# Four of ten expert blocks per group added on chip by 0/1 products instead of by a scatter to DRAM

## The reference, cut to what matters

```python
act = silu(einsum('nd,edf->nef', t, w_gate_e)) * einsum('nd,edf->nef', t, w_up_e) * gates[:, :, None]
routed = einsum('nef,efd->nd', act, w_down_e)           # 64 experts, inner width 256, 8 gates per token not zero
x = x + gate_ffn * (routed + shared)                    # then a last RMSNorm
```

## Time and profile before

| what | value |
|---|---|
| median of 3 executions | 1000.14 us (999.35 to 1002.08) |
| profiled execution, its own time | 997.12 us |
| its span | 995.4 us |
| PE busy | 873.0 us (88%) |
| DVE, ACT, POOL busy | 340.7, 249.2, 157.0 us |
| moved by DMA | 299.40 MB, mean 301 GB/s |
| `gate_up` of turn 11 / turn 39 starts | 527.19 us / 951.03 us |

### The profile page before, as it was taken

One profiled execution on the slowest core, in us unless ns is written; L12 is line 12 of the kernel. 1 busy time (PEld: TensorE's weight loads), 2 busy tenths in 40 slices (PEclk: granted clock), 3 DMA queues, 4 the chain that ended last, 5 costly groups with the idle time before them and its releaser, 6 DMA issues.

```text
span 995.4 us, 11581 instructions
## 1 busy us (share of the span) xinstructions
PE 873.0 (88%) x4026; PEld 495.0 (50%) x4026; DVE 340.7 (34%) x833; ACT 249.2 (25%) x415; POOL 157.0 (16%) x210
## 2 busy tenths in 40 slices
PE   4799998999999899999987787978979888978974
PEld 2388876899888744443333332423324333433321
DVE  1653572766674552332321212111112121212125
ACT  2546623444233411112110111111101111111111
POOL 7200000000010500221221111111212212212212
PEclk9799999999999999999997989978979998989998
DMA  9974887232346688899999999999999999999924
GB/s 344 348 272 149 290 299 172 86 105 85 108 137 234 247 343 305 301 358 380 405 388 408 374 376 391 356 369 387 359 376 368 378 383 384 363 375 391 385 65 190
DMA packets 87048, 299.40 MB, mean 301 GB/s; under 512 B 18181, under 2 KB 34625, under 8 KB 62048
## 3 DMA queue, kind: packets, MB, share of 16 engines
q1 hardware_dynamic: 64400, 263.21, 67.0%
q0 software_dynamic: 13904, 31.13, 11.6%
q10 hardware_dynamic: 8704, 4.54, 1.9%
HBM read 287.16 MB, written 29.10 MB: 318 GB/s over the span
## 4 chain that ended last, share of the span: by engine, by line
PE 48%; DMA 37%; SPq 5%; DVE 4%; issue 2%; ACT 2%; POOL 1%; ACTq 1%; POOLq 0%; DVEq 0%
DMA gu<-in_w_up_e_dram 33%; PE bank L1423 14%; PE bank L1047 6%; PE bank L1049 6%; PE bank L1048 6%; PE bank L1442 4%; SPq L484 4%; DMA chunk_raw<-in_w_ada_dram 3%; PE bank L1316 2%; PE bank L1075 2%; PE bank L1116 1%; DMA y_dram<-y_sb,slot_row 1%; SPq L495 1%; PE bank L1411 1%; PE bank L1149 1%
## 5 line engine op out<-in xcount | busy, mean ns | idle before, releaser
L1423 PE MATMUL bank<-gu,x_t 128*64 128x512 f32 (+1 forms) x1024 | 311.3, 654 | 72.3 <-DMA gu<-in_w_up_e_dram 70.6
L1423 PEld LDWEIGHTS bank<-gu,x_t 128*64 128x64 f32 (+1 forms) x1024 | 109.7, 163 | 242.2 <-issue 215.7
L1442 PE MATMUL bank<-dn,a_t 128*64 128x512 f32 (+1 forms) x512 | 145.3, 597 | 4.8 <-ACT shared_sb L982 3.5
L719 POOL DMA_INDIRECT y_dram<-y_sb,slot_row x39 | 62.7, 1608 | 463.3 <-issue 237.8
L1904 DVE TENSOR_TENSOR act_sb<-silu_sb,bank 128x256 f32<-128x256 f32 x40 | 16.9, 422 | 323.8 <-ACT silu_sb L1017 323.8
L1017 ACT ACTIVATE silu_sb<-bank 128x256 f32<-128x256 f32 x40 | 15.4, 385 | 344.3 <-PE bank L1423 344.3
L1442 PEld LDWEIGHTS bank<-dn,a_t 128*64 128x64 f32 (+1 forms) x512 | 48.5, 150 | 74.8 <-issue 67.5
L1047 PE MATMUL bank<-h_hi,chunk_lo 128*128 128x384 f32 x240 | 84.6, 353 | 0.0
L1008 ACT ACTIVATE y_sb<-bank,slot_gate 128x512 f32<-128x512 f32 x80 | 50.7, 684 | 126.1 <-PE bank L1442 103.2
L1049 PE MATMUL bank<-h_hi,chunk_hi 128*128 128x384 f32 x240 | 81.1, 338 | 0.0
L1048 PE MATMUL bank<-h_lo,chunk_hi 128*128 128x384 f32 x240 | 80.8, 337 | 0.0
(11 more groups left out here) (336 smaller groups left out, 939.4 us busy)
## 6 DMA issues: line engine op xcount, KB each, us to landing
gu<-in_w_gate_e_dram SPq DMA_DIRECT2D x64, 1024.0 KB, 16.0
gu<-in_w_up_e_dram SPq DMA_DIRECT2D x64, 1024.0 KB, 28.2
dn<-in_w_down_e_dram SPq DMA_DIRECT2D x64, 1024.0 KB, 27.2
chunk_raw<-in_w_ada_dram SPq DMA_DIRECT2D x24, 1024.0 KB, 8.6
chunk_raw<-in_w_in_dram SPq DMA_DIRECT2D x18, 1024.0 KB, 5.3
chunk_raw<-in_w_out_dram SPq DMA_DIRECT2D x4, 1024.0 KB, 5.0
y_dram<-zeros POOLq DMA_DIRECT2D x1, 3072.0 KB, 18.0
chunk_raw<-in_w_pa_dram SPq DMA_DIRECT2D x2, 1024.0 KB, 5.0
```

Of the source, the lines that this page charges most:

```text
L719: pool.indirect_dma_start(y_dram[:, :], bass.IndirectOffsetOnAxis(ap=slot_row[:, u % UN:u % UN + 1], axis=0), y_sb[u % 2][:, :], None, bou ...
L1423: mm = pe.matmul(bank[2 + u % 2][at_x, :].rearrange("p (g n) -> p g n", g=2), x_t[:, cols], wide[:, :, k, :], start=(k == 0), stop=(k == K ...
L1442: mm = pe.matmul(bank[5 + half][at_x, :], a_t[:, cols], dn[slot_of(x, first)][:, wc], start=(k == 0), stop=(k == 1))
```

## The change

In the three later groups the blocks u = 0, 2, 5 and 7 (`PLACED`) are no longer scattered: 12 blocks of 40. In the turn after such a block, behind everything else of that turn, DVE makes its 0/1 matrix `place_t` in one operation over 384 columns (it compares `tok_no`, the numbers 0 to 383, with the block's `slot_val`). PE waits for it, then runs six products `place_t` x `y_sb` into six accumulator banks, and DVE adds each of the six banks to `ffn_acc`, three tiles of 128x1024 in SBUF. PE's next `gate_up` waits for the first of these additions, `turn_tokens` after it for the sixth. POOL fills `ffn_acc` with zeros and makes `tok_no` in the last turn of the first group. After the loop, DVE multiplies each tile of `ffn_acc` by `gate_ffn` and adds it to `x_sb`, six operations of 128x1024 in a row, ahead of L1926. The counts in the waits on `added` follow: 27 scatters instead of 39. The semaphores of the three RMS steps are merged into `squares_summed` and `rstd_made`, with counts that keep each wait as it was (left out below).

```diff
+PLACED = (0, 2, 5, 7)
+SCATTERED = BPG - len(PLACED)
...
+        tok_no = at("tok_no", [P, NTOK], EX + 113.5)
+        ffn_acc = [at(f"ffn_acc{t}", [P, D], EX + 48 + 4 * t) for t in range(TT)]
...
+        def is_placed(u, first):
+            return not first and u % UN in PLACED
+        def scatters_ahead(b, u):
+            back = 1 if u < 0 else 0
+            return b * (16 * SCATTERED) + 16 * (len(PLACED) - SCATTERED * back + sum(v not in PLACED for v in range(u % UN)))
+        def places_ahead(b, v, each):
+            return b * (each * len(PLACED)) + each * (PLACED.index(v) - len(PLACED))
+        def place_outs(u):
+            return [(0, 0, bank[2 + (u + 1) % 2]), (1, 0, bank[0]), (2, 0, bank[1]), (0, 1, bank[4]), (1, 1, bank[5]), (2, 1, bank[6])]
...
-            sp.wait_ge(S["added"], passes * (NPASS_BLK * 16) - 16)
+            sp.wait_ge(S["added"], passes * (NGRP * SCATTERED * 16) + 16 * (len(PLACED) - 1))
...
# POOL, block_turn
                     gather(i + 2, u + 2)
-                    if not (first and u == 0):
-                        scatter(i - 1, u - 1)
+                    if first and u == UN - 1:
+                        pool.wait_ge(S["x2_ready"], TT)
+                        for t in range(TT):
+                            pool.memset(ffn_acc[t][:, :], 0.0).then_inc(S["zero_filled"], 1)
+                        count(tok_no[:, :], [[1, NTOK]], 0).then_inc(S["zero_filled"], 1)
+                    if not (first and u == 0) and not (u and is_placed(u - 1, first)):
+                        scatter(i - 1, u - 1, 16 * (i - 1) if first else scatters_ahead(b, u - 1))
...
# PE
+            def place(v, b):
+                i, at_y = b * UN + v, v % 2
+                outs = place_outs(v + 1)
+                halves = [slice(0, 512), slice(512, 1024)]
+                pe.wait_ge(S["x_first"], i + 3)
+                pe.wait_ge(S["x_second"], i + 3)
+                pe.wait_ge(S["a_ready"], i + 2)
+                pe.wait_ge(S["place_made"], places_ahead(b, v, 1) + 1)
+                for n, (t, half, out) in enumerate(outs):
+                    if n == 0:
+                        pe.wait_ge(S["y_half"], places_ahead(b, v, 1) + 1)
+                    elif n == 3:
+                        pe.wait_ge(S["y_ready"], i + 1)
+                    pe.matmul(out[:, :], place_t[:, t * P:(t + 1) * P], y_sb[at_y][:, halves[half]],
+                              start=True, stop=True).then_inc(S["place_mm"], 1)
# PE, block_turn
+                    after_place = u >= 2 and is_placed(u - 2, first)
+                    if after_place:
+                        pe.wait_ge(S["place_out"], places_ahead(b, u - 2, 6) + 1)
                     gate_up(u, b, first)
+                    if after_place:
+                        pe.wait_ge(S["place_out"], places_ahead(b, u - 2, 6) + 6)
                     turn_tokens(i + 1, u + 1, first)
...
                     block_rows(i + 3, u + 3)
+                    if u and is_placed(u - 1, first):
+                        place(u - 1, b)
...
# DVE, at the end of block_turn's turn
+                    if u and is_placed(u - 1, first):
+                        place_rows(u - 1, b)
+            def place_rows(v, b):
+                dve.tensor_scalar(place_t[:, :], tok_no[:, :], slot_val[:, v:v + 1], float(EMPTY),
+                                  ALU.subtract, ALU.is_equal).then_inc(S["place_made"], 1)
+                for n, (t, half, out) in enumerate(place_outs(v + 1)):
+                    cols = slice(512 * half, 512 * half + 512)
+                    dve.wait_ge(S["place_mm"], places_ahead(b, v, 6) + n + 1)
+                    dve.tensor_tensor(ffn_acc[t][:, cols], ffn_acc[t][:, cols], out[:, :], ALU.add).then_inc(S["place_out"], 1)
...
             block_turn(0, True)
+            dve.wait_ge(S["zero_filled"], 7 + TT + 1)
             with dve.Fori(1, passes * NGRP) as b:
                 block_turn(b, False)
+            dve.wait_ge(S["place_out"], passes * (NGRP * 6 * len(PLACED)) - 6 * len(PLACED))
+            for t in range(TT):
+                go(dve.tensor_tensor(ffn_acc[t][:, :], ffn_acc[t][:, :], gate_ffn[:, int(t > 0), :], ALU.mult))
+                go(dve.tensor_tensor(x_sb[:, t, :], x_sb[:, t, :], ffn_acc[t][:, :], ALU.add))
```

More of the change, by code:

```diff
@@ L400, in hybrid_step @@
         assert [SLOT0[x] for x in turns[False][-1]] == [SLOT[x] for x in turns[False][-1]]
+        assert max(PLACED) < UN - 2 and all(v + 1 not in PLACED for v in PLACED)
+        def is_placed(u, first):
[7 more added lines that the diff above has]
+            return [(0, 0, bank[2 + (u + 1) % 2]), (1, 0, bank[0]), (2, 0, bank[1]), (0, 1, bank[4]), (1, 1, bank[5]), (2, 1, bank[6])]
         def rows_of(x, order_x):
@@ L578, in _, with rms @@
             pool.memset(xr_pad[:, :, RC + 2:RC + 3], 0.0).then_inc(S["zero_filled"], 1)
-            def rms(n, summed):
+            def rms(n):
                 for t in range(TT):
-                    pool.wait_ge(summed, t + 1)
+                    pool.wait_ge(S["squares_summed"], TT * n + t + 1)
                     at_t = rstd[:, n, t:t + 1]
                     go(pool.tensor_scalar(at_t, sumsq[:, n, t:t + 1], 1.0 / D, EPS, ALU.mult, ALU.add))
-                    pool.tensor_tensor(at_t, at_t, minus_half[:, 0:1], ALU.pow).then_inc(S[f"rstd{n + 1}"], 1)
+                    pool.tensor_tensor(at_t, at_t, minus_half[:, 0:1], ALU.pow).then_inc(S["rstd_made"], 1)
             pool.wait_ge(S["consts"], 3)
-            rms(0, S["sumsq1"])
+            rms(0)
             go(pool.memset(fold[:, :], 0.0))
@@ L709, in gather, with scatter @@
                                         bounds_check=NTOK - 1, oob_is_err=False).then_inc(gathered[u % 2], 16)
-            def scatter(i, u, first=False):
+            def scatter(i, u, ahead, first=False):
                 pool.wait_ge(S["y_ready"], i + 1)
@@ L716, in scatter @@
                 if not (isinstance(i, int) and i == 0):
-                    pool.wait_ge(S["added"], 16 * i)
+                    pool.wait_ge(S["added"], ahead)
                 pool.sem_inc(S["pool_turn"], 1)
@@ L741, in _ @@
                 pool.sem_inc(S["pool_turn"], 1)
-            rms(2, S["sumsq3"])
+            rms(2)
         @block.scalar
@@ L760, in squares @@
                                    accum_out=sumsq[:, n, t:t + 1]).then_inc(signal, 1)
-            squares(0, xhat, S["sumsq1"])
+            squares(0, xhat, S["squares_summed"])
             act.wait_ge(S["cond_loaded"], 80)
@@ L999, in x_copy, with rows_out @@
                 act.activation(x_t[:, 0:512], bank[0][:, :], ACT.Copy).then_inc(S["x_first"], 1)
-            def rows_out(i, u, done):
+            def rows_out(i, u, done, free, place=False):
                 act.wait_ge(S["dn_used"], done)
@@ L1005, in rows_out @@
                 if not (isinstance(i, int) and i <= 1):
-                    act.wait_ge(S["added"], 16 * (i - 1))
+                    act.wait_ge(S["added"], free)
                 for half in range(2):
@@ L1009, in rows_out, with buffer_free @@
                                          scale=slot_gate[:, u:u + 1])
+                    if place and half == 0:
+                        ins.then_inc(S["y_half"], 1)
                 ins.then_inc(S["y_ready"], 1)
+            def buffer_free(b, u):
+                return scatters_ahead(b, u - 2) + (0 if (u - 2) % UN in PLACED else 16)
             def block_turn(b, first):
@@ L1023, in block_turn @@
                     if not (first and u == 0):
-                        rows_out(i - 1, (u - 1) % UN, experts[0] if first else b * EPG + experts[0])
+                        rows_out(i - 1, (u - 1) % UN, experts[0] if first else b * EPG + experts[0],
+                                 16 * (i - 2) if first else buffer_free(b, u - 1), u and is_placed(u - 1, first))
             x_copy(0)
@@ L1029, in _ @@
                 block_turn(b, False)
-            rows_out(passes * NPASS_BLK - 1, UN - 1, passes * NE)
+            rows_out(passes * NPASS_BLK - 1, UN - 1, passes * NE, buffer_free(passes * NGRP - 1, UN - 1))
             for t in range(TT):
@@ L1504, in _ @@
             for t in range(TT):
-                dve.wait_ge(S["rstd1"], t + 1)
+                dve.wait_ge(S["rstd_made"], t + 1)
                 normalise(0, t, xhat, S["xhat1"])
@@ L1700, in normalise2 @@
             def normalise2(t):
-                dve.wait_ge(S["rstd2"], t + 1)
+                dve.wait_ge(S["rstd_made"], TT + t + 1)
                 normalise(1, t, xhat2, S["xhat2"])
@@ L1943, in _ @@
             for t in range(TT):
-                dve.wait_ge(S["rstd3"], t + 1)
+                dve.wait_ge(S["rstd_made"], 2 * TT + t + 1)
                 dve.scalar_tensor_tensor(x_sb[:, t, :], x_sb[:, t, :], rstd[:, 2, t:t + 1], final_g_sb[:, :],
```

12 lines of the change are left out of this document (6 added, 6 removed).

## The result

The changed kernel takes **1014.71 us** (median of 4, 1013.27 to 1017.54) against 1000.44 us for the kernel before, timed beside it (median of 4, 999.35 to 1002.08): a ratio of 1.0145, 95% interval 1.0119 to 1.0171. It is 14.3 us slower. The forecast was 1018 us, in the range 1003 to 1033. The profiled execution took 1013.27 us, with a span of 1011.5 us.

A forecast was written before the change was run, and what follows sets the result against it. Weights bound the kernel, PE close behind; the change makes PE the bound. Loop +1.7, clock +10.2 and tail +6.1 give +18.0 us on 997.1, 1015.1; with 3.0 us to the median, 1018 us, range 1003 to 1033.

The forecast's parts named there:

- What bounds the loop: Loop: weights bound it before, PE close behind; with the change PE has no wait left from turn 12 on.
- the signs that were named: Trace signs: 2.1 us pauses, 5.2 us products, near-zero weight waits, DMA share well under 0.97, low clock behind pauses, later tail.
- Price of a placed block: On PE in the turn after each placed block: 2.1 us wait plus 5.2 us products, 7.3 us; twelve cost 87.6.
- The rival in which weights stay the bound: Loop: below 5.6 us per placed block everything fits PE's holes, the loop ends 19 us earlier, 987 us; chance 0.07.
- The sum of the loop: Turns 12 to 38: 324 us work plus 87.6 us placing against 409.9, +1.7 us, then +10.2 us for the clock.
- the clock's term: Loop: PE's clock falls behind the new pauses, 6 x 1.7 = +10.2 us, with ends 0 and 20.4.
- a fall in half of them: Loop: six of the twelve new PE pauses are followed by a clock fall costing 1.7 us each.
- The scatters' relief: DMA queues: twelve scatters fewer at 1.6 us each let the last weights come 19 us earlier (14 to 24).
- the lone scatter's 2.0: DMA queues: upper end of a scatter's cost, from one scatter running alone, 2.0 us.
- the price under load: DMA queues: a scatter's cost taken from a full group, 1.6 us each, with half the bytes at the gather's price.
- the holes: PE, turn 12 to 39: 61.5 us idle for weights plus 24.4 us low clock, 85.9 us to hide new work.
- The tail: After the loop: last products start 3.8 us later behind DVE's six operations, plus 2.3 us low clock, +6.1 us.

The follow-up runs named there:

- the two experiments with the scatters: Changed kernel without placing, 12 scatters still out: 975.72 us; changed kernel with all 39 scatters back, 12 blocks counted twice: 1016.34 us.
- other executions with the same pauses: Changed kernel with the six operations after the last block's matrix (eight falls): 1012.68 us; changed kernel with all 39 scatters back (five): 1016.34 us.
- with six placed blocks: Changed kernel with only blocks 2 and 7 of each later group placed, matrix still late: 1003.34 us, ratio 1.0019.
- the early matrix: Changed kernel with place_t made before DVE's wait for transposed activations, and PE's a_ready wait moved to the fourth product: 989.46 us.
- the scatters out: Changed kernel without products, 0/1 matrices, additions and the six operations after the loop; the 12 scatters stay out too: 975.72 us, ratio 0.9749.

## Why the prediction was right

**What bounds the loop: right.** PE does from turn 12 on, with no wait for weights; the chain, the waits and the two experiments with the scatters say so alike. Of the signs that were named only the DMA share is weak: 0.94 in the loop, where "well under 0.97" was said.

**Price of a placed block: right.** 7.23 us at nine blocks and 7.40 at three, against 7.3 forecast: 1.88 or 2.08 us from the end of the lookup to the products (2.1 was forecast), and 5.35 or 5.32 from their start to the next `gate_up` (5.2). The rival in which weights stay the bound needed less than 5.6 us. The Trainium skill's page "TensorE: Matmul & The Clock Gate", section "Back-to-back issue gap", gives about 216 ns as the gap of an isolated product of 512 columns; an estimate from it, six products, is 1.3 us, and the trace does not agree. The Trainium skill's page "FP8 and Floating Point Precision", section "TensorE Precision Notes", says that true FP32 takes four passes; an estimate from both, 24 passes of 216 ns, is 5.2 us, and the trace agrees with 5.35.

**The sum of the loop: mechanism right, size of the clock's term too large.** The 27 turns without the placed blocks take 322.2 us in the trace (forecast 324), the placed blocks 9 x 7.23 + 3 x 7.40 = 87.3 (87.6), and four falls of 1.7 are 6.8 (10.2): 416.3 us, which is what the trace has from the lookup's end in turn 11 to turn 39 (543.83 to 960.15). Before it was 409.2 (541.85 to 951.03): +7.1 us where 1.7 + 10.2 = +11.9 was forecast. The term most at fault is "a fall in half of them": four, not six, in the profiled execution, 3.4 of the 4.8 us. Each cost 1.70 us, as taken. How many there would be was a guess: other executions with the same pauses had eight of twelve and five of twelve, and with six placed blocks six of six.

**The scatters' relief: undersized, without effect.** 2.1 us for each, not 1.6; the working had the lone scatter's 2.0 as its upper bound and took the price under load. The step that fell short is that it counted packets alone: the shorter waits are 17.2 us, 1.4 for each scatter, and another 8.0 us are PE's low clock, which the working had among the holes but not in the relief. Most of it lies idle in the changed kernel, so the time is hardly touched. How much of it the early matrix needs for its gain was not tested.

**The tail: the sum is near, one term is missing.** +7.0 us where +6.1 was forecast. The last products start 3.6 us later (forecast 3.8), and DVE's first addition behind them comes 30.56 us after turn 39 instead of 25.89: +4.7, so the low clock cost 1.1, not 2.3. The remaining 2.35 us lie behind DVE's last operation, where I had nothing. It ends 3.7 us before the span's end before (991.68, 995.4) and 6.0 us after (1005.45, 1011.5); this is its row in the kernel before:

```profile
990.40 1.28 DVE L1945 SCALAR_TENSOR_TENSOR x_sb<-x_sb,rstd,final_g_sb 128x1024 f32<-128x1024 f32 x1 [0.72 <-POOL rstd L586]
```

**The median.** On the profiled execution +18.0 us was forecast and +16.1 of span came: 4.8 too much in the loop, 0.9 too little in the tail, and 2.0 ahead of turn 12 (541.85 to 543.83) that no term stands for. The rest of the 3.3 us between 1018 and 1014.71 is the frame: the profiled execution lies 1.4 us under its median, and I had carried over the 3.0 of the kernel before. So a term too large and two that were missing partly cancel; the mechanism was right, but that the sum came out this near is in part luck.

## What to carry to other kernels

Taking load from the resource that bounds a loop pays only up to the point at which the next engine becomes the bound; after that each microsecond put on that engine counts in full, pauses included. So look first at what the new work waits for: here the place of one 0.4 us operation in DVE's order, with one wait on PE, was worth 25 us (1014.71 to 989.46; 22.4 of them are seen in the loop), and it decided between 1.4% slower and 1.0% faster. Work that nobody waits for soon, like the epilogue here, belongs behind the operation that another engine is waiting for.

## What the hardware showed that was not expected

- **Equal pauses, unequal clocks.** Of twelve pauses of 1.9 to 2.1 us, four in one execution, eight in another and five in a third were followed by a fall of the granted clock (0.79 over 8 us in the one shown); with six placed blocks all six were. Each fall cost 1.7 us. With twelve pauses of 0.65 us it stayed at 1.00 over the whole loop. What makes the difference between equal pauses is open.
- **The end of the program depends on the scatters.** From DVE's last operation to the end of the span it took 3.7 us before, and 6.0 us in the changed kernel. With all 39 scatters back and everything else as changed (1011.25 to 1014.9) it took 3.65 us. In the trace the difference lies in POOL's last instruction, a DRAIN. It takes 5.35 us in both kernels with 39 scatters, 8.1 us in both with 33, 8.0 us with 30, and 7.7 us in all those with 27, whether they place blocks or not. So it follows the number of POOL's indirect DMAs, but not evenly. Why is open, and it was not tested by itself.
- **A scatter that accumulates cost more time than its packets.** The 12 scatters' relief was 2.1 us each. The packets of queue 0 took 11.6% of 995.4 us before and 9.9% of 979.8 us with the scatters out: 18.5 us less, 1.5 us for each, near the forecast's 1.6. The difference of 7.2 us is near the 8.0 us by which PE's busy time for the same work fell, behind fewer and shorter waits (15 instead of 19, the longest 5.7 instead of 7.2 us). That this is the cause was not tested by itself.
